# Shared weight slabs, layer-norm sums as four columns, and a split za product in a two-block network kernel on one core

## The reference

```python
def layer_norm(x, g, b):
    mu = jnp.mean(xf, -1, keepdims=True)
    var = jnp.mean(jnp.square(xf - mu), -1, keepdims=True)
    return (xf - mu) * lax.rsqrt(var + LN_EPS) * g + b
def modulate(x, shift, scale):
    return x * (1 + scale[:, None, :]) + shift[:, None, :]
```

## Time and profile before

| | us |
|---|---|
| median of 3 runs | 3978.22 (3974.04 to 3982.32) |
| the profiled execution's own time | 3979.66 |
| its span, first to last instruction | 3978.4 |
| TensorE busy | 3738.8 (94%) |
| granted TensorE clock, mean | 0.971 of full |

### The profile page before, as it was taken

The page is one execution under the profiler, slowest core; times in us unless marked ns, Lnnn a source line. Parts: engine busy times, 40 slices in busy tenths (PEclk is TensorE's granted clock), DMA queues, the critical chain, the costliest instruction groups (busy, mean ns, idle before and its releaser), DMA issues.

```text
span 3978.4 us, 53300 instructions
## 1 busy us (share of the span) xinstructions
PE 3738.8 (94%) x20996; PEld 3112.3 (78%) x20996; DVE 2195.4 (55%) x3743; ACT 1492.0 (38%) x2561; POOL 1060.1 (27%) x707
## 2 busy tenths in 40 slices
PE   8999999989999999898999889899999989799999
PEld 7889768788889888757878867678878867578777
DVE  6556773576667777746432679831154337840442
ACT  3223554453225223444322423342234324353352
POOL 0002103232014101303201422843211333254224
PEclk9999999999999999999999999899999999899999
DMA  7565424246655565303332411112111112112112
GB/s 294 171 202 158 129 95 138 96 138 193 226 179 155 181 195 163 109 33 117 126 97 88 131 38 54 48 35 67 48 38 36 60 49 74 64 46 96 56 43 95
DMA packets 132151, 433.92 MB, mean 109 GB/s; under 512 B 14784, under 2 KB 14912, under 8 KB 131520
## 3 DMA queue, kind: packets, MB, share of 16 engines
q1 hardware_dynamic: 131904, 430.52, 33.5%
HBM read 428.36 MB, written 2.10 MB: 108 GB/s over the span
## 4 chain that ended last, share of the span: by engine, by line
PE 77%; DVE 13%; ACT 4%; issue 3%; DMA 1%; POOL 1%; SPq 0%; DVEq 0%; ACTq 0%; POOLq 0%
PE ps L633 21%; PE ps L634 21%; PE ps L635 21%; DVE cut L2229 4%; PE ps L1923 1%; DVE cut L559 1%; PE ps L1800 1%; PE ps L1900 1%; PE ps L1884 1%; ACT cut L549 1%; PE ps L1906 1%; PE ps L1888 1%; PE ps L631 1%; PE ps L659 1%; PE ps L661 1%
## 5 line engine op out<-in xcount | busy, mean ns | idle before, releaser
L633 PE MATMUL ps<-cut 128*128 128x512 f32 (+1 forms) x5312 | 1892.8, 356 | 109.7 <-DVE cut L559 25.2
L634 PE MATMUL ps<-cut 128*128 128x512 f32 (+1 forms) x5312 | 1856.3, 349 | 0.0
L635 PE MATMUL ps<-cut 128*128 128x512 f32 (+1 forms) x5312 | 1854.3, 349 | 0.0
L633 PEld LDWEIGHTS ps<-cut 128*128 128x128 f32 x5312 | 1022.4, 192 | 273.9 <-issue 107.5
L634 PEld LDWEIGHTS ps<-cut 128*128 128x128 f32 x5312 | 1024.2, 193 | 130.0 <-issue 5.1
L635 PEld LDWEIGHTS ps<-cut 128*128 128x128 f32 x5312 | 1022.4, 192 | 126.4
L559 POOL TENSOR_TENSOR cut<-cut 128x1024 fp32r<-128x1024 f32 (+3 forms) x280 | 604.4, 2162 | 1336.7 <-ACT cut L549 1336.1
L549 ACT ACTIVATE cut<-cut 128x1024 fp32r<-128x1024 f32 (+3 forms) x680 | 632.1, 938 | 768.8 <-PE ps L635 670.8
L559 DVE TENSOR_TENSOR cut<-cut 128x1024 fp32r<-128x1024 f32 (+3 forms) x400 | 481.0, 1205 | 440.7 <-ACT cut L549 440.7
L932 POOL TENSOR_TENSOR cut<-cut 128x512 fp32r<-128x512 f32 (+1 forms) x100 | 148.0, 1480 | 1087.6 <-ACT cut L891 1087.6
L2229 DVE SCALAR_TENSOR_TENSOR cut<-cut,cols 128x512 f32<-128x512 f32 (+1 forms) x330 | 283.0, 858 | 11.7
(11 more groups left out here) (314 smaller groups left out, 3539.5 us busy)
## 6 DMA issues: line engine op xcount, KB each, us to landing
cut<-in_ffn_in SPq DMA_DIRECT2D x200, 512.0 KB, 4.1
cut<-in_mod_w SPq DMA_DIRECT2D x136, 512.0 KB, 4.3
cut<-in_ffn_out SPq DMA_DIRECT2D x96, 384.0 KB, 3.3
cut<-in_ffn_out SPq DMA_DIRECT2D x96, 320.0 KB, 3.0
cut<-in_w_ada SPq DMA_DIRECT2D x48, 512.0 KB, 3.5
cut<-in_w_merge SPq DMA_DIRECT2D x48, 512.0 KB, 3.4
cut<-in_even_in SPq DMA_DIRECT2D x36, 512.0 KB, 3.6
cut<-in_proj SPq DMA_DIRECT2D x48, 256.0 KB, 2.6
```

What stands on the lines that cost most here:

```text
L633: te.matmul(o, hi[:, k - ka, w], xs[0], start=k == 0, stop=False)
L634: te.matmul(o, hi[:, k - ka, w], xs[1], start=False, stop=False)
L635: ins = te.matmul(o, lo[:, k - ka, w], xs[0], start=False, stop=last)
```

## The change

What it does:

- **Slabs stay.** The B halves of gu, ob, oi and oo get no slabs of their own (`again`): they use those of A, which are released by B's groups. For that the 8 slabs need 8 places: the ring of five (oi, which has 4 slabs, gets the ring of five too) or, for oo, the ring of three, and side places in memory that is free at that time (`SIDE`). A side place is free from the last slab before the product on. The patterns of `low` change: gu A "vg", ob "vg", fo B "gv", oo "v".
- **Norm sums.** GpSimd also adds the squares of tiles 0 to 5 (`pool_square`). `pe_ln` makes the square the stationary operand: eight fp32 matmuls (two token blocks times four terms) with 4 columns of `pick` leave mean and mean square with tokens on the partitions, 128 x 4. VectorE's chain runs on 128 x 2, and `pe_ln_spread` brings 1/std and mean/std back to 128 x 512 in PSUM by four fp32 matmuls against the identity, from inside group 1 of the half (tile 5 of 8, or 6 of 11). `dve_ln` reads both from PSUM.
- **Squares one group later.** `act_square` of tile m-1 stands in group m, after the root and the rounding of the norm.
- **za.** The weights are split into a rounded part and a rest side by side, and the product is 16 fp32r matmuls of 128 x 512; rows 0 to 15 and 16 to 31 are added by the next product, over 32 rows.
- **Order.** q0 and q1 move from `QK` to between oa(0) and za, and `rows_in` gives no rows to q0, q1, g6 and g7 and two each to k0 to k3.

```diff
     def ahead(self, m):
         last, n = self.first(m) + len(self.cuts) - 1, self.first(m)
+        end = self.slab0 + len(self.mgs) * len(self.cuts)
+        if self.again:
+            n = end - 1
         def room(i):
             plain = i >= NRAW and not SLABS[i - NRAW].lin.split and i - NRAW >= last
-            return not plain and (SLABS[i].before is None or SLABS[i].before < last)
+            freed = self.slab0 if self.stays and i >= end else last
+            return not plain and (SLABS[i].before is None or SLABS[i].before < freed)
...
 def low_in(name):
-    return {"B": "vg"}.get(name[-1], "v")
+    return {"A": "vg"}.get(name[-1], "v")
 def low_out(name):
-    return {"A": "v", "B": "ggv"}.get(name[-1], "v")
+    return {"A": "v", "B": "gv"}.get(name[-1], "v")
...
 for _x in PLAN:
+    if _x.again:
+        LIN[_x.again].stays, _x.slab0 = True, LIN[_x.again].slab0
+        for _i in range(len(_x.mgs)):
+            SLABS[_x.slab0 + _i].release = ("p_mm", _x.name, _i)
+        continue
...
+SIDE = {"gu": (5, 6, 7), "ob": (8, 6, 5), "oo": (3, 4, 9, 10, 11)}
+            side = SIDE.get(name[0], ()) if s.lin.stays else ()
+            nring = 8 - len(side)
+            if side and j >= nring:
+                s.slot, s.before = side[j - nring], s.lin.slab0 - 1
+            else:
+                more = [3, 4] if name[0] in ("gu", "fo", "ob", "oi") else []
...
 def act_tail(name, tag, nxt):
         for part in ab(*name):
             def epilogue(m):
-                if part[-1] == "B" and m:
+                if part[-1] == "B":
                     yield from act_ln(tag, "A", m)
-                yield from act_square(part, tag, m)
+                if m:
+                    yield from act_square(part, tag, m - 1)
...
+    def pool_square(tag, h, t):
+        acc = squares(tag, h)
+        ge.wait_ge(*(yield "a_sq", tag, h, t))
+        if t > 1:
+            ge.wait_ge(*(yield "g_sq", tag, h, t - 1))
+        ge.tensor_tensor(acc, acc if t > 1 else square(tag, h, 0), square(tag, h, t), ALU.add).then_inc(*sig("g_sq", tag, h, t))
...
     def pe_ln(tag, h):
-        for t in (NT - 2, NT - 1):
-            yield from pe_square(tag, h, t)
-        yield from pe_sum([(total, ("g_total", tag, h, 7))], ones, 256, ("v_mean", tag, h), ("p_mean", tag, h))
+        parts = [(squares(tag, h), ("g_sq", tag, h, 5), 3)]
+        parts += [(square(tag, h, t), ("a_sq", tag, h, t), 3) for t in (NT - 2, NT - 1)] + [(total, ("g_total", tag, h, NT - 1), 1)]
+        for i, (x, key, o) in enumerate(parts):
+            te.wait_ge(*(yield key))
+            for j in range(2):
+                ins = te.matmul(PS[b][:, 0:4], x[:, 128 * j:128 * j + 128], pick[:, o - j:o - j + 4], start=i == 0 and j == 0,
+                                stop=i == 3 and j == 1)
+    def pe_ln_spread(tag, h):
+        b = bank["p_spread", tag, h] = yield from pe_take(("v_nrm", tag, h, NT - 1))
+        kept.add(b)
+        te.wait_ge(*(yield "v_mr", tag, h))
+        for i in range(4):
+            ins = te.matmul(PS[b][:, 128 * i:128 * i + 128], ln_stats(h)[:, i:i + 1].to_broadcast([128, 128]), ident,
+                            start=True, stop=True)
...
-            ve.tensor_tensor(x, x, rstd, ALU.mult).then_inc(*sig("v_cen", tag, h, t))
+            ve.tensor_tensor(x, x, PS[bank["p_spread", tag, h]][:, 0:256], ALU.mult).then_inc(*sig("v_cen", tag, h, t))
...
             if k0 == 0:
                 kept.difference_update(rest)
+                for h in range(2):
+                    yield from pe_linear(("q", h), urhs, ALLG, lambda m, gi: ("a_lin", ("q", h)), none)
                 yield from pe_za()
...
-    QK = [("q", 0), ("k", 0), ("q", 1), ("k", 1)]
+    QK = [("k", 0), ("k", 1)]
     def pe_za():
-                ins = te.matmul(PS[b][0:16, :], wz[:, k * 16:(k + 1) * 16], x[:, k, :].bitcast(F32),
-                                start=k == 0 and c == 0, stop=k == NT - 1 and c == 1)
+                ins = te.matmul(PS[b][:, :], WZS[:, 32 * k:32 * k + 128], x[:, k, :], start=k == 0 and c == 0,
+                                stop=k == NT - 1 and c == 1)
```

More of the change, by code:

```diff
@@ L217, in place_slabs @@
         if s.lin.split:
[L218 to L222, removed]
+            name, j = s.lin.name, n - s.lin.slab0
+            side = SIDE.get(name[0], ()) if s.lin.stays else ()
[4 more added lines that the diff above has]
+                more = [3, 4] if name[0] in ("gu", "fo", "ob", "oi") else []
+                ring = [0, 1, 2] + (more or ([5] if name == ("glu", 0) else []))
+                i = (i + 1) % len(ring)
+                s.slot, s.before = ring[i], holds.get(ring[i])
+            holds[s.slot] = n
+            if name == ("oo", "A") and j == 7:
+                i = SLABS[s.lin.slab0].slot - 1
 place_slabs()
@@ L605, in pe_weights, with pe_linear @@
         te.wait_ge(*(yield low_of(n) if SLABS[n].lin.split else raw_of(n)))
-    def pe_linear(name, x, groups, until, ready, after=None, beside=None, ms=None, take=None, gis=None):
+    def pe_linear(name, x, groups, until, ready, after=None, beside=None, ms=None, take=None, gis=None, within=None):
         L = LIN[name]
@@ L628, in pe_linear @@
                                 te.wait_ge(*(yield key))
+                        if within and (m, k) == within[0]:
+                            yield from within[1]
                         xs, last = x(k, g), k == L.kt - 1
@@ L859, in pe_ffn @@
                 after = (lambda m: pe_ln(u, "B") if m == 0 else nothing(m)) if gu[-1] == "A" else None
+                within = ((1, 5), pe_ln_spread(u, "B")) if gu[-1] == "A" else None
                 yield from pe_linear(gu, urhs, [g], lambda m, gi: (("a_sil", "v_hid")[m % 2], gu, m), ready, after,
-                                     ms=range(begun, LIN[gu].groups))
+                                     ms=range(begun, LIN[gu].groups), within=within)
             ready = lambda k, gi: [hl_of(l, f, half, k)]
@@ L974, in after @@
                     yield from pe_ln(tag, "A")
-                if m > 1:
-                    yield from pe_square(tag, h, m - 2)
-            yield from pe_linear(part, x, [HALF[h]], lambda m, gi: ("v_z", part, m), ready if h == "A" else none, after)
+            yield from pe_linear(part, x, [HALF[h]], lambda m, gi: ("v_z", part, m), ready if h == "A" else none, after,
+                                 within=((1, LIN[part].kt * 5 // 8), pe_ln_spread(tag, "A")) if h == "B" else None)
         if not nxt:
             yield from pe_ln(tag, "B")
+            yield from pe_ln_spread(tag, "B")
     def act_tail(name, tag, nxt):
@@ L1043, in square, with squares, square_read @@
         return ttmp(tag)[t % 2][:, HALF[h][0]:HALF[h][1]]
-    def pe_square(tag, h, t):
-        if t == 0 and tag == "f00" and h == "A":
-            te.wait_ge(*(yield "d_const",))
-        if t == 0:
-            if spent:
-                kept.discard(spent.pop())
-            b = bank["p_var", tag, h] = yield from pe_take(("v_var", tag, h))
-            kept.add(b)
-        te.wait_ge(*(yield "a_sq", tag, h, t))
-        te.matmul(PS[bank["p_var", tag, h]][:, 0:256], ones, square(tag, h, t), start=t == 0, stop=t == NT - 1).then_inc(*sig("p_var", tag, h, t))
+    def squares(tag, h):
+        return ttmp(tag)[2][:, HALF[h][0]:HALF[h][1]]
+    def square_read(tag, h, t):
+        return ("g_sq", tag, h, max(t, 1))
     def act_square(part, tag, t):
@@ L1365, in dve_rg @@
             if k0 == 0:
+                yield from dve_linear(("q", 0), nothing)
                 yield from decay(7)
@@ L1368, in dve_rg @@
                 yield from low(6)
+                yield from dve_linear(("q", 1), nothing)
                 yield from low(7)
@@ L1378, in pool_rg @@
             yield from pool_linear(("ga", t), nothing)
-        for k0 in (0, 4):
-            yield from pool_linear(("oa", k0), nothing)
+        for name in (("oa", 0), ("q", 0), ("q", 1), ("oa", 4)):
+            yield from pool_linear(name, nothing)
     def sp_rg():
```

132 lines of the change are left out of this document (85 added, 47 removed).

## The result

The changed kernel takes 3949.9 us (median of 4, 3947.2 to 3951.9) against 3979.7 us before on the same chip: a ratio of 0.9927, 95% interval 0.9909 to 0.9944. That is 29.8 us less, where 58 were forecast. Its profiled execution took 3947.17 us with a span of 3945.5.

The account below looks back on a forecast made before the run. TensorE, busy for 94% of the span, was taken as the bound. Terms −11.2 −10 −37 +3 −1 −2 = −58.2 us against 3979.7 gave 3921.5, forecast as 3920 us (3900 to 3940; wider range 3885 to 3958).

Parts of the forecast that it names:

- Part 1: Layer-norm sums: with the square as stationary operand, 2.95 us a half, 35.4 us instead of 46.6, 11.2 us less.
- Part 2: za product: 32 fp32 instructions of 13.84 us become 16 fp32r matmuls of 3.8 us, 10 us less.
- part 4: GLA and odd ends: mod rows 3 us more, earlier split of z 1 us less, last norm 2 us less.
- Part 3 (b): B halves of the four feed-forward outputs: waits of 21.3 us in all fall to 2 us each.
- (a): B halves of ob and oo: waits of 5.0 and 8.6 us fall to 0.5 us each.
- Part 3 (d): gu behind ob and oo: waits of 4.3 and 8.6 us fall to 1 us each.
- (e): gu behind a feed-forward tail: a loss, waits growing from 4.3 to 10 us with the root behind splits.
- Part 3 (c): Starts of xa and oi: waits of 10.1 and 11.1 us on VectorE's norm chain fall to 5 each.
- The 5 us of spread elsewhere: Waits at the spread outside gu behind a feed-forward tail: 0.5 us a time, 5 us added.
- GpSimd holds VectorE up: Rival: 30 additions in B halves each stretch a VectorE step by 1.0 us, 30 us, 3950 us; chance 0.09.
- Only the matmuls get cheaper: Rival: waits of VectorE's norm chain only move from place to place, 3957 us; chance 0.14.
- every wait goes: Rival: no loss in gu behind feed-forward tails and VectorE keeps up in the tails, 3884 us; chance 0.12.

Follow-up runs that it names:

- experiment 2: Changed kernel with the old layer-norm sums back (matmuls of ones, one per square, no squares added on GpSimd): 3956.86 us, ratio 0.9954.
- kernel 4: Changed kernel with splits limited to slab 3 at the first group of gu, the rest behind the square root: 3940.68 us, ratio 0.9908.
- kernel 5: Changed kernel with sums, root and spread of norm B one group later in the three gu products: 3943.79 us, ratio 0.9912.
- 7: Changed kernel with gu's norm B one group later and splits limited to slab 3 for the first two groups: 3930.78 us, ratio 0.9882.
- experiment 8: Changed kernel with all low halves of the A products of gu and oi subtracted on VectorE, none on GpSimd: 3940.99 us, ratio 0.9902.
- experiment 11: Changed kernel with gu's sums and spread one group later, splits behind the root for two groups, A's low halves on VectorE: 3916.24 us, ratio 0.9844.

## Why the prediction was half right

The sign, the order of the effects in the tails and the range held; the size did not. Of the forecast 58 us some 25.7 did not come (58.2 against 32.5 in the profiled executions). Step by step:

*Part 1, the matmuls: price right, account too large.* Undisturbed, and start to start, the 16 short sums take 1.71 us and the 8 of the spread 0.81 to 0.89, against 1.70 and 0.87. But a late square doesn't cost 0.43 us everywhere: in an A half six of them went, and 2.34 us came in f00, f01 and f10, 2.1 in ob, 1.1 in oo and 0.2 in f11, where TensorE waits for other things. That is 10.5 us of 15.5. The last norm, put at 2 us less, is 1.2 us longer: with nothing beside it, TensorE waits 1.2, 2.8 and 2.4 us between the terms of the sums and 1.7 at the spread.

*Part 2 and part 4:* 13.84 us became 3.72, and the stretch with GLA is 8.6 us shorter where −10, +3 and −1 gave 8. So close a fit is partly luck: the stretch takes 346.0 us in the changed kernel and 342.0 to 349.4 in the variants that leave za alone.

*Part 3 (b):* 36.7, 36.7, 36.7 and 36.4 us, where the terms give 31.7 + 2.95 + 2 = 36.7. *(a)* 25.65 and 25.71 where 26.5 were due, right in time. Both reasons that it gave are real, but their weights were not asked for: the table under experiment 2 shows that in ob the stops for squares made most of these waits, and in oo squares and slabs.

*Part 3 (d), the failed step:* "Since the ring takes five of the eight slabs before the tail ends, 1 us each is left." The windows were to be 50.1 us (46.1 of products, 2.95 of norm, 1 of wait) and are 58.8 and 56.8: 15.6 us. It looked only at TensorE's need for slabs. The B half in front had become 6 to 10 us shorter, and the norm of A on VectorE and the additions on GpSimd, once hidden by TensorE's stops, now end behind it, and with them the last residuals, squares and totals. And the root on which the spread waits was behind three splits and their subtractions here as well, not only behind f01. Experiments 4, 5, 7 and 8 take these apart, and with all of them out of the way (experiment 11) two of the three windows are 48.6 us. *(e)* was foreseen as a loss, with its mechanism (four splits in front of the root, seen at 1229.60 to 1237.57; wait of 4.5 us at the spread); 61.5 us came for 59.1.

*Part 3 (c):* the starts of xa and oi were to fall to 31 us and are 33.4 and 36.5, 7.9 us missing. This is one of the things that was to show me wrong, and does. In oi TensorE waits 2.2 and 1.4 us at the sums and 1.7 for the last step of VectorE's norm chain (L1172, the subtraction that gives the rest). The window is some 2 us shorter with the low halves on VectorE (34.2 us) and with splits twice (34.5). In xa there is no stop at the sums, but 4.1 us for L1172 and 0.8 at the spread: the chain of VectorE, as forecast, but for longer. No experiment cleared these four groups, so the cause in (c) is read from waits alone.

*The 5 us of spread elsewhere* came, but not on top: of 12.0 us of waits at the spread, 7.3 lie in the starts of gu, 3.1 in xa and in three B halves of fo (0.7 to 0.8 each), and 1.7 in the last norm. All are within lengths that are already compared here, so the term drops out.

The terms: 15.6 + 2.4 + 7.9 for (d), (e), (c), less 1.7 for (a) and 5 for the spread, make 19.2; 5.0 of the A halves and 1.5 of the last norm (its terms together gave −0.35) make 25.7. What is left, GLA, the stretches behind oi and the last norm, and the prologue, comes to nearly nothing.

*The rivals.* "GpSimd holds VectorE up" gave 3950 us, the time that was measured, but by 30 us of stretched steps, and experiment 8 puts 9 us on GpSimd's subtractions alone. I had put it at nothing. The copy at 851.10, which reads PSUM, took 0.15 us beside GpSimd; the step behind it, with both operands in SBUF, 2.13 us until GpSimd ended. By the Trainium skill (SBUF — State Buffer, "SBUF: two separate sides") whoever has the port pair shared by VectorE and GpSimd holds it for a whole instruction, and the other waits. The trace agrees to 0.01 us (853.41 and 853.40). And of 89 steps that read the spread from PSUM while GpSimd worked none took over 0.42 us, where the 14 scalings behind them that met GpSimd (L1209, in SBUF) took 1.31 us on the mean, against 0.41. "Only the matmuls get cheaper" gave 3957, and its reason is the one that most of the failure has: a wait goes from one place to the next. Of "every wait goes", 3884 us, kernel 11 shows a part, at 3916.

## What to carry to other kernels

A wait removed in one stretch brings the next meeting point forward: ask which engine sets it, and whether its work got shorter too. Work that is put ahead "because a place is free" goes into the same queue as the small steps on which the busiest engine waits; bound how far ahead it may run there. And price an edit with its neighbours' edits: kept slabs are worth nothing in one version and 10 to 20 us in the next.

## What the runs showed that was not expected

The half clock outlasts the stop and costs about as much. Windows of TensorE behind ob in the changed kernel (length; busy; granted clock; DMA): before the stop, the stretch with sums and 15 products, the spread with the products next to it, and later.

```profile
835.00:842.90 7.90, 7.90 (x69) 1.00 0.42 135
...
846.35:854.60 8.25, 6.95 (x31) 0.50 0.38 120
854.69:857.50 2.81, 2.81 (x13) 0.50 0.58 201
860.00:870.00 10.00, 10.00 (x86) 1.00 0.01 2
```

Behind the stop of 3.2 us the granted clock is 0.50, the level of 1.2 GHz: the sums take 3.4 us rather than 1.7. In kernel 4, without a stop at the spread, the 15 products behind them still take 3.35 us; in kernel 11, without any stop here, 1.87, at a granted clock of 1.00 (2.4 GHz). In the three starts TensorE's waits at sums and spread are 4.6, 8.2 and 3.8 us, and the starts are 10.2, 12.8 and 8.2 us longer than the 25.6 of a start without any (kernel 11): here a stop is to be counted one and a half to two times. No run separates the clock from the stop.

A square root moved behind an activation of another function cost two table loads of 1.28 us rather than one (kernel 5).
